# One transfer per cache page instead of two, in a hybrid decoder step with paged latent attention

## The chip, the cores and the metric

The kernel runs on one core of a Trainium2 chip. Times are device microseconds (us) of one execution. The median of three runs of the kernel before is 3482.98 us (3482.84 to 3485.76). The five engines are TensorE (PE), VectorE (DVE), ScalarE (ACT), GpSimd (POOL) and SyncE (SP, which here only issues transfers); all transfers run on the core's 16 DMA engines.

## The reference, cut to what matters

One decoder layer serves a prompt of 1024 tokens and 8 sample sequences of one new token each. The prompt and the samples share all weights. After the mixer comes an expert retrieval: every token picks 128 of 16384 experts, and a row of 1024 floats is gathered for each pick from two tables (`expert_u`, `expert_v`). The part that the change touches is the samples' attention over their cache:

```python
past_ckv = cache_ckv[l, page_table].reshape(dec_b, past, KV_RANK)      # 16 pages of 128 keys, 256 floats each
past_kr = cache_krope[l, page_table].reshape(dec_b, past, QK_ROPE)     # the same keys, 64 floats each
s = (jnp.einsum('bqhr,bkr->bhqk', q_lat, ckv)
     + jnp.einsum('bqhp,bkp->bhqk', q_rope, kr)).astype(jnp.float32) * SM_SCALE
p = jax.nn.softmax(s, axis=-1)
o_lat = jnp.einsum('bhqk,bkr->bqhr', p, ckv)
```

Each of the 8 samples has 16 pages of 128 keys, scattered in a pool by `page_table`; all data are float32.

## The kernel before, in words

**The backbone.** The expert retrieval of the 8 prompt tiles (128 tokens each) is the long work. Each tile has 32 groups of 4 picks, so there are 256 groups. For a group GpSimd issues 4 gathers into `u_ring` and 4 into `v_ring` (L1854, each 128 rows of 4 KB; each ring has 8 slots), VectorE forms 4 dot products (L1737), ScalarE the gelu and four diagonals (L1223), and TensorE adds the weighted rows up in 16 matmuls (`v_group`, L925). A gather waits until its slot is free: `u_free` comes from VectorE's dot product, `v_free` from TensorE's matmuls.

**The front work.** All else (projections, attention, mixing, top-k of the next tile or of the samples) is cut into stages. `make_plan` spreads them over the groups by a table of costs; every engine's program has the same order. The samples are the last unit: their stages lie in groups 195 to 249. Of these, 36 are stages of `pages`, numbered n, four for each sample b (a quarter of its pages each) and four to drain. A stage of pages n = 4b + q works on TensorE like this: scores of the quarter before (L840, L841), `page_turn` (transposes of the quarter's 4 pages, L862 for the latents and L863 for the rope keys), the scores turned (L853), and, where q is 2, `page_values` of the sample before (L879 to L884), whose end is the event `page_pv`. VectorE and ScalarE copy the transposed pages out (L1524, L1525, L1157). In a group with stages of pages, VectorE does two of the group's four dot products ahead of the stage and two behind it, and TensorE does one stage ahead of its `v_group`. Some groups have two stages.

**The loads.** SP issues all page loads in order (`load_page`, L534 to L538): it reads the page number from `page_table_sb` into a register and issues the transfers. Even and odd samples have different homes. For sample 0 the 16 latent pages are loaded early, when the prompt's attention is over; its 16 rope pages go to `w_ukT`, which the samples' own queries still need, and so they are issued only once `qlat_kept`, `q_roped`, `conv_done` and `conv_stored` have come. Then follow samples 1 to 7, each with 16 pages of two transfers, 128 rows of 1024 bytes and 128 rows of 256 bytes; sample b waits for `page_pv` of sample b - 2, which had the same home. `page_turn` waits for a whole quarter:

```python
pe.wait_ge(pages_loaded[b % 2][q], (b // 2 + 1) * 2 * QP * 16)
```

The homes before are `ckv_rows` and `ckvT` (latents, even samples), `w_ukT` (rope keys, even samples) and `work` (odd samples, latents and rope keys apart). Behind the page loads SP has the weights of the samples' output and query projections.

Of the kernel before, what the change touches and what calls it, by code (L numbers as in the profile page):

```python
# [26 lines left out]
P = 128  # L27
# [3 lines left out]
TILES = SEQ // P  # L31
SB = 8
PAGE = 128
NPAGES = 16
# [3 lines left out]
ROPE = 64  # L38
QR = 384
KV = 256  # L40
# [31 lines left out]
QP = NPAGES // QUARTERS  # L72
# [189 lines left out]
def build(nc, a, out):  # L262

    with ExitStack() as ctx:
        def sb(name, shape, dt=F32):
            return ctx.enter_context(nc.sbuf_tensor(name, shape, dt))
# [5 lines left out]
        pages_loaded = [[ctx.enter_context(nc.semaphore(f"pages_loaded{i}{q}")) for q in range(QUARTERS)] for i in range(2)]  # L272
# [3 lines left out]
        F = [ctx.enter_context(nc.psum_tensor(f"front{i}", [P, 512], F32)) for i in range(6)]  # L276

        ident = sb("ident", [P, P])
# [9 lines left out]
        w_uq = sb("w_uq", [P, QR // P, H, NOPE + ROPE])  # L288
        w_ukT = sb("w_ukT", [P, H, KV])
# [3 lines left out]
        ckv_rows = sb("ckv_rows", [P, TILES, KV])  # L293
        ckvT = sb("ckvT", [P, 2, SEQ])
# [16 lines left out]
        work = sb("work", [P, 5 * D])  # L311
# [38 lines left out]

        second_keys = [W[1][:, h * 256:(h + 1) * 256] for h in range(4)] + [mix_raw[:, h * 256:(h + 1) * 256] for h in range(1, 4)] + [W[2][:, 256:512]]

        prompt_keys = [ckv_rows[:, :, :], ckvT[:, :, :].rearrange("p c (n r) -> p (c n) r", r=KV)]
        pages_kr = [w_ukT[:, :, :].rearrange("p h (n r) -> p (h n) r", r=ROPE),
                    work[:, NPAGES * KV:NPAGES * (KV + ROPE)].rearrange("p (n r) -> p n r", r=ROPE)]

        def page_rows(b, n):
            if b % 2:
                return work[:, n * KV:(n + 1) * KV]
            return prompt_keys[n // TILES][:, n % TILES, :]  # L360

        pages_T = rows_next[:, :, :].rearrange("p a b -> p (a b)")[:, 0:3 * 512].rearrange("p (c k) -> p c k", c=3)

# [82 lines left out]
        def _(sp):  # L446
# [19 lines left out]
            r = 0  # L466
            for name in ("g_mix_norm", "g_q", "g_kv", "g_attn_out", "g_conv_out"):
                n = a[name].shape[1] // P
# [5 lines left out]
            def load_rope(u):  # L474

                after(sp, on.q_roped, UNITS[u][0])
                row, T = UNITS[u][0] * P, width(u)
                sp.dma_start(cos_t[:, 0:T], a["c_rope"][0, :, row:row + T]).then_inc(on.rope_loaded, 16)
                sp.dma_start(sin_t[:, 0:T], a["c_rope"][1, :, row:row + T]).then_inc(on.rope_loaded, 16)
# [50 lines left out]
                load_unit_start(u)  # L530
                load_unit_rest(u)

            def load_page(b, n, what):
                page = sp.value_load(page_table_sb[0:1, b * NPAGES + n:b * NPAGES + n + 1], min_val=0,  # L534
                                     max_val=a["cache_ckv"].shape[1] - 1)
                for dst, src in what:
                    sp.dma_start(dst, a[src][0, bass.ds(page, 1)].rearrange("a k r -> k (a r)"))\
                        .then_inc(pages_loaded[b % 2][n // QP], 16)  # L538


            sp.wait_ge(on.olat_kept, TILES * H)
            sp.wait_ge(on.pages_table_loaded, 16)
            for n in range(NPAGES):
                load_page(0, n, [(page_rows(0, n), "cache_ckv")])
            load_rope(SAMPLE)
            load_unit_start(SAMPLE)
            for k in range(CONV, N_IN + WR):
# [4 lines left out]
            sp.wait_ge(on.q_roped, TILES + 1)  # L552
            sp.wait_ge(on.conv_done, SAMPLE + 1)
            sp.wait_ge(on.conv_stored, 3 * 16)
            for n in range(NPAGES):
                load_page(0, n, [(pages_kr[0][:, n, :], "cache_krope")])
            for b in range(1, SB):

                if b >= 2:
                    sp.wait_ge(on.page_pv, b - 1)  # L560
                for n in range(NPAGES):
                    load_page(b, n, [(page_rows(b, n), "cache_ckv"), (pages_kr[b % 2][:, n, :], "cache_krope")])
            for k in range(N_IN + WR, PIECES):
                load_w(SAMPLE, k)

# [12 lines left out]
        def _(pe):  # L578
# [277 lines left out]

            def page_turn(n):
                b, q = divmod(n, QUARTERS)
                pe.wait_ge(pages_loaded[b % 2][q], (b // 2 + 1) * 2 * QP * 16)
                for pg in range(QP):  # L860
                    for c in range(2):
                        nc.tensor.transpose(F[c][:, pg * P:(pg + 1) * P], page_rows(b, q * QP + pg)[:, c * P:(c + 1) * P], ident[:])  # L862
                    last = nc.tensor.transpose(F[2][0:ROPE, pg * P:(pg + 1) * P], pages_kr[b % 2][:, q * QP + pg, :], ident[:])  # L863
                last.then_inc(on.page_turned, 1)

            def own_key_scores():
# [21 lines left out]
            def pages_stage(n):  # L888

                b, q = divmod(n, QUARTERS)  # L890
                if n == 0:
                    own_key_scores()
                if q == 1 and b:
                    pe.wait_ge(on.page_max_made, 2 * b - 1)
                    nc.tensor.transpose(F[5][0:H, 0:P], small_col(C_PM, 4), ident[:]).then_inc(on.page_gmax, 1)
                if 0 < n <= SB * QUARTERS:
                    page_scores(n - 1)
                if n < SB * QUARTERS:
                    page_turn(n)
                if q == 1 and b:  # L900
                    pe.wait_ge(on.page_max_made, 2 * b)
                    nc.tensor.matmul(F[5][:, 128:132], gm_rows[:], ident[0:H, 0:H], start=True, stop=True)\
                        .then_inc(on.page_gmax_spread, 1)
                if 0 < n <= SB * QUARTERS:
                    page_scores_turn(n - 1)
                if q == 2 and b:
                    page_values(b - 1)
                if q == 3 and b:
                    pe.wait_ge(on.value_rows_kept, b)
                    for c in range(2):  # L910
                        last = nc.tensor.matmul(F[5][:, COLS_VALUES + 4 * c:COLS_VALUES + 4 * c + 4],
                                                value_rows[:, c * P:(c + 1) * P], pick_values[:], start=True, stop=True)
                    last.then_inc(on.values_turned, 1)
# [124 lines left out]
            for t in range(SB):  # L1038
                pe.wait_ge(v_loaded[t], (TILES * (GROUPS // 2) + 1) * 16)
                for q in range(4):  # L1040
                    last = nc.tensor.matmul(acc[32 * q:32 * q + SB, 0, 0:256], s_fan[:, t, :], v_ring[:, t, q * 256:(q + 1) * 256],
                                            start=(t == 0), stop=(t == SB - 1))
# [910 lines left out]
```

## Time and profile before

| | |
|---|---|
| median of three runs | 3482.98 us |
| the profiled execution | 3482.97 us |
| its span, first to last instruction | 3481.2 us |
| busy: PE, DVE, POOL, ACT | 72%, 65%, 66%, 24% |
| moved by DMA | 1279.47 MB in 368,936 packets, mean 368 GB/s |
| mean granted TensorE clock | 0.83 of full speed |
| first transfer into a home of a page | 2436 us |
| first rope page of sample 0 issued | 2771.5 us |
| last page values (`page_values` of sample 7) done | 3153.6 us |

The span is what the engines' instructions cover; the 1.8 us between it and the execution's own time lie around it. A packet of the DMA view is one row of a transfer (4 KB for a gather, 1024 or 256 bytes for a page) or one write of a semaphore, 16 of them for each transfer.

### The profile page before, as it was taken

How to read it: one execution, taken by the hardware profiler on the slowest of the kernel's cores; microseconds unless marked ns; L12 is line 12 of the kernel's file. 1: busy time of each engine (PE TensorE's matmuls, PEld its weight loads, DVE VectorE, ACT ScalarE, POOL GpSimd, SP SyncE). 2: the span in 40 equal slices, each digit the busy share in tenths (PEclk: the TensorE clock that was granted, in tenths of full speed). 3: DMA queues.
4: the chain of work that ended last, by engine and by line, in shares of the span. 5: the costliest groups of instructions: out<-in, count | busy, mean ns of one | idle time of the engine just before them, and what ended most of it. 6: DMA issues, size and time to landing. Idle time of an engine off the chain costs nothing.

```text
span 3481.2 us, 38789 instructions
## 1 busy us (share of the span) xinstructions
PE 2504.6 (72%) x11520; PEld 1399.3 (40%) x11520; DVE 2277.3 (65%) x5456; ACT 823.2 (24%) x2065; POOL 2291.3 (66%) x2068
## 2 busy tenths in 40 slices
PE   7558764977874497788854878878655888877764
PEld 6425432644541154444511544445213534432421
DVE  3685588467588955665898557657897254454784
ACT  2112222233222121332212213322112122232111
POOL 0467566666567775676777777676677576557675
PEclk9878878999987798899976999989876688888676
DMA  6699999998999999999999999999999999999998
GB/s 239 234 400 365 354 404 372 353 365 307 403 370 359 372 388 382 327 359 407 409 374 384 388 411 357 329 411 410 403 356 383 361 368 353 342 341 403 411 409 339
DMA packets 368936, 1279.47 MB, mean 368 GB/s; under 512 B 59372, under 2 KB 77974, under 8 KB 353368
## 3 DMA queue, kind: packets, MB, share of 16 engines
q0 software_dynamic: 297216, 1082.26, 81.2%
q1 hardware_dynamic: 62324, 168.67, 12.6%
q10 hardware_dynamic: 9188, 26.05, 2.3%
q8 instruction: 95, 1.56, 0.2%
q14 instruction: 113, 0.93, 0.1%
HBM read 1262.31 MB, written 13.48 MB: 366 GB/s over the span
## 4 chain that ended last, share of the span: by engine, by line
DVE 36%; PE 35%; DMA 13%; issue 7%; ACT 4%; POOL 2%; SPq 2%; DVEq 0%; ACTq 0%; POOLq 0%
DVE u_ring L1737 14%; PE acc L925 11%; PE front L587 10%; DMA u_ring<-in_expert_u,pick_cur 6%; PE front L803 3%; DMA v_ring<-in_expert_v,pick_cur 2%; DVE si_u L1604 2%; DVE sv L1603 2%; PE front L712 2%; PE front L735 2%; DVE work L1604 2%; DMA w_ukT<-in_cache_krope 1%; DVE work L1603 1%; DVE work L1648 1%; DVE work L1650 1%
## 5 line engine op out<-in xcount | busy, mean ns | idle before, releaser
L925 PE MATMUL acc<-v_ring,diag 128*64 128x512 f32 x4096 | 1176.1, 723 | 623.1 <-ACT diag L1223 354.7
L1854 POOL DMA_INDIRECT u_ring<-in_expert_u,pick_cur x1024 | 1144.0, 1117 | 576.8 <-issue 293.4
L1854 POOL DMA_INDIRECT v_ring<-in_expert_v,pick_cur x1024 | 1130.6, 1104 | 587.8 <-PE acc L925 313.3
L1737 DVE CUSTOM_DVE_ANT_0 u_ring<-u_ring,xn_cur 128x1024 f32<-128x1024 f32 x1024 | 1209.6, 1221 | 318.3 <-DMA u_ring<-in_expert_u,pick_cur 302.7
L925 PEld LDWEIGHTS acc<-v_ring,diag 128*64 128x64 f32 x4096 | 347.8, 165 | 1328.7 <-issue 905.6
L1223 ACT ACTIVATE diag<-ident,wgt 128x64 f32<-128x64 f32 x1024 | 272.3, 337 | 759.4 <-DVE wgt L1743 707.9
L587 PE MATMUL front<-work,w_ring 128*128 128x256 f32 (+2 forms) x1536 | 308.9, 343 | 25.2 <-DVE mo L1596 14.5
L587 PE MATMUL front<-mo,w_ring 128*128 128x256 f32 (+2 forms) x1536 | 304.2, 339 | 0.0
L587 PEld LDWEIGHTS front<-work,w_ring 128*128 128x128 f32 x1536 | 254.2, 204 | 77.1 <-issue 36.1
L1216 ACT ACTIVATE gelu<-dots 128x4 f32<-128x4 f32 x256 | 52.5, 205 | 922.8 <-DVE dots L1737 922.7
L587 PEld LDWEIGHTS front<-mo,w_ring 128*128 128x128 f32 x1536 | 259.0, 205 | 22.6
L803 PE MATMUL front<-w_ring,work 128*128 128x256 f32 (+1 forms) x512 | 120.2, 396 | 18.5 <-DVE work L1569 14.2
L1603 DVE MAX8 sv<-work 128x8 f32<-128x128 f32 (+1 forms) x252 | 72.5, 288 | 84.3 <-ACT work L1201 27.3
L1524 DVE COPY rows_next<-front 128x512 f32<-128x512 f32 x32 | 22.1, 691 | 141.2 <-PE front L863 141.2
L803 PEld LDWEIGHTS front<-w_ring,work 128*128 128x128 f32 (+1 forms) x512 | 93.9, 186 | 50.8 <-DVE work L1569 15.9
L1216 ACT ACT_TABLE_LOAD x85 | 109.1, 1283 | 1.5
L735 PE MATMUL front<-work,ckv_rows 128*128 128x128 f32 x560 | 79.9, 305 | 26.3 <-DVE work L1508 26.3
L735 PEld LDWEIGHTS front<-work,ckv_rows 128*128 128x128 f32 x560 | 74.2, 215 | 39.1 <-DVE work L1508 32.4
L1737 DVE DVE_READ_ACCUMULATOR2_ANT dots<- 128x1 f32 x1024 | 82.8, 81 | 0.0
L712 PE MATMUL front<-ckvT,rows_next 128*128 128x512 f32 (+3 forms) x176 | 72.6, 537 | 9.2 <-DVE q_ro L1425 5.8
L1604 DVE FIND_INDEX8 si_u<-sv,work 128x8 uint32<-128x128 f32 (+1 forms) x252 | 71.5, 284 | 0.6 <-issue 0.6
L1603 DVE MAX8 work<-mo 128x8 f32<-128x256 f32 (+1 forms) x144 | 61.4, 426 | 15.5 <-DVE mo L1625 0.9
(303 smaller groups left out, 2329.1 us busy)
## 6 DMA issues: line engine op xcount, KB each, us to landing
w_ring<-in_w_pieces SPq DMA_DIRECT2D x112, 1024.0 KB
u_ring<-in_expert_u,pick_cur POOLq DMA_INDIRECT x1024, 10.1
v_ring<-in_expert_v,pick_cur POOLq DMA_INDIRECT x1024, 9.1
x_t<-in_x_prompt SPq DMA_DIRECT2D x16, 512.0 KB
v_ring<-in_w_pieces SPq DMA_DIRECT2D x8, 1024.0 KB, 11.9
work<-in_cache_ckv SPq DMA_DIRECT2D x64, 128.0 KB
xn_cur<-scratch ACTq DMA_DIRECT2D x14, 512.0 KB, 10.0
scratch_x<-rows_next ACTq DMA_DIRECT2D x8, 512.0 KB
```

The costliest lines, as they stand in the source:

```text
L587: last = nc.tensor.matmul(dst, w[:, k, c0:c0 + m], x_chunks(k // 4)[:, (k % 4) * T:(k % 4 + 1) * T], start=(k == 0), stop=(k == DC - 1))
L712: nc.tensor.matmul(dst, q_lat[:, c, h, :], ckvT[:, c, ks], start=(c == 0), stop=False)
L735: last = nc.tensor.matmul(F[4][:, c * P:(c + 1) * P], ckv_rows[:, j, c * P:(c + 1) * P], W[1][:, j * P:(j + 1) * P], start=(j == 0), stop= ...
L803: last = nc.tensor.matmul(dst, mixed[i][:, k * T:(k + 1) * T], w[:, k, :], start=(k == 0), stop=(k == DC - 1))
L925: last = nc.tensor.matmul(acc[rows, half, :], diag[:, s % RING, :], v_ring[:, s % RING, half * 512:half * 512 + 512], start=(s < 2), stop= ...
L1216: nc.scalar.activation(gelu[:, g * G:(g + 1) * G], dots[:, g * G:(g + 1) * G], ACT.Gelu).then_inc(on.gelu_done, 1)
L1223: nc.scalar.activation(diag[:, s % RING, :], ident2[:], ACT.Copy, scale=wgt[:, s:s + 1]).then_inc(on.diag_made, 1)
L1603: own(v.max(best, scores), held=True)
L1604: last = v.max_index(index[:, 8 * r:8 * r + 8], best, scores)
L1648: own(v.tensor_tensor(hit[0:T], pos_f[0:T, c, hs].unsqueeze(3).to_broadcast(grid), iota16[0:T].unsqueeze(1).unsqueeze(1).to_broadcast(grid ...
L1737: v.tensor_tensor_reduce(u_ring[:, slot, :], u_ring[:, slot, :], xn2_cur[:, block_of(r), :], 1.0, 0.0, ALU.mult, ALU.add, dots[:, g * G + ...
L1854: pool.indirect_dma_start(ring[:, slot, :], None, a[table][0], bass.IndirectOffsetOnAxis(ap=pick, axis=0)).then_inc(loaded[slot], 16)
```

## The change

The host lays `cache_ckv` and `cache_krope` side by side in one input `cache_rows`, so that a key's 256 latents and 64 rope values are one row of 1280 bytes. A page is then one transfer of 128 such rows. In the core's memory a page takes 320 columns. Odd samples have all 16 in `work`. Even samples have six in `ckv_rows`, six in `ckvT` and four in `w_uq`. The first twelve pages of sample 0 are loaded early; its last four wait for the events that the rope pages waited for. The bytes are the same.

```diff
+        PAGE_COLS = KV + ROPE
+        HELD_PAGES = TILES * KV // PAGE_COLS
+        page_homes = [ckv_rows[:, :, :].rearrange("p n r -> p (n r)"), ckvT[:, :, :].rearrange("p c t -> p (c t)"),
+                      w_uq[:, :, :, :].rearrange("p c h n -> p (c h n)")]
+
+        def page_at(b, n):
+
+            if b % 2:
+                return work[:, n * PAGE_COLS:(n + 1) * PAGE_COLS]
+            home, k = divmod(n, HELD_PAGES)
+            return page_homes[home][:, k * PAGE_COLS:(k + 1) * PAGE_COLS]
...
-            def load_page(b, n, what):
+            def load_page(b, n):
                 page = sp.value_load(page_table_sb[0:1, b * NPAGES + n:b * NPAGES + n + 1], min_val=0,
-                                     max_val=a["cache_ckv"].shape[1] - 1)
-                for dst, src in what:
-                    sp.dma_start(dst, a[src][0, bass.ds(page, 1)].rearrange("a k r -> k (a r)"))\
-                        .then_inc(pages_loaded[b % 2][n // QP], 16)
+                                     max_val=a["cache_rows"].shape[0] - 1)
+                sp.dma_start(page_at(b, n), a["cache_rows"][bass.ds(page, 1)].rearrange("a k r -> k (a r)"))\
+                    .then_inc(pages_loaded[b % 2][n // QP], 16)
...
-            for n in range(NPAGES):
-                load_page(0, n, [(page_rows(0, n), "cache_ckv")])
+            for n in range(2 * HELD_PAGES):
+                load_page(0, n)
...
-            for n in range(NPAGES):
-                load_page(0, n, [(pages_kr[0][:, n, :], "cache_krope")])
+            for n in range(2 * HELD_PAGES, NPAGES):
+                load_page(0, n)
...
-                    load_page(b, n, [(page_rows(b, n), "cache_ckv"), (pages_kr[b % 2][:, n, :], "cache_krope")])
+                    load_page(b, n)
...
-                pe.wait_ge(pages_loaded[b % 2][q], (b // 2 + 1) * 2 * QP * 16)
+                pe.wait_ge(pages_loaded[b % 2][q], (b // 2 + 1) * QP * 16)
...
+    arrays["cache_rows"] = np.concatenate([arrays["cache_ckv"][0], arrays["cache_krope"][0]], axis=2)
```

`page_rows` and `page_kr` are now the first 256 and the last 64 columns of `page_at`. No matmul, copy or wait of another engine changes in kind or number.

## Rows read from the trace of the kernel before

**Rows 1.** The page's 40 slices (87 us each) of the whole execution

```profile
DMA  6699999998999999999999999999999999999998
GB/s 239 234 400 365 354 404 372 353 365 307 403 370 359 372 388 382 327 359 407 409 374 384 388 411 357 329 411 410 403 356 383 361 368 353 342 341 403 411 409 339
```

**Rows 2.** Busy time by stretch: us, busy us and count per engine, PEclk, DMA, GB/s

```profile
2771.00:3153.00 382.00, 304.56 (x1623) 145.94 (x1620) 191.60 (x403) 102.45 (x244) 244.53 (x219) 0.84 0.98 352
3200.00:3400.00 200.00, 135.93 (x574) 65.34 (x574) 145.69 (x390) 34.33 (x112) 140.64 (x132) 0.72 1.03 410
```

**Rows 3.** DMA view, 3200 to 3400 us

```profile
DMA packets 21224, 82.06 MB, mean 410 GB/s; under 512 B 2365, under 2 KB 2365, under 8 KB 20060
```

**Rows 4.** DMA view, 2855 to 2867 us, with two queues

```profile
DMA packets 2233, 4.73 MB, mean 395 GB/s; under 512 B 726, under 2 KB 1237, under 8 KB 2231
...
q0 software_dynamic: 1116, 4.07, 86.6%
q1 hardware_dynamic: 1115, 0.65, 17.8%
```

**Rows 5.** DMA view, 2780 to 2784 us, then 2444 to 2448 us

```profile
DMA packets 820, 1.59 MB, mean 397 GB/s; under 512 B 456, under 2 KB 456, under 8 KB 820
...
DMA packets 688, 1.59 MB, mean 397 GB/s; under 512 B 69, under 2 KB 379, under 8 KB 687
```

**Rows 6.** DMA view, 2771 to 3153 us

```profile
DMA packets 66219, 134.44 MB, mean 352 GB/s; under 512 B 23732, under 2 KB 38068, under 8 KB 66189
...
q0 software_dynamic: 31197, 113.62, 79.3%
```

**Rows 7.** DMA view, 2831 to 2843 us, then 3023 to 3035 us

```profile
DMA packets 1043, 3.81 MB, mean 317 GB/s; under 512 B 114, under 2 KB 114, under 8 KB 1043
...
DMA packets 1074, 1.88 MB, mean 157 GB/s; under 512 B 427, under 2 KB 703, under 8 KB 1073
```

**Rows 8.** Waits, 2771 to 3153 us: engine line waited for: us, times, longest

```profile
POOL u_ring L1854 <- DVE dots L1737: 57.8, 11, 8.4
PE front L862 <- DMA w_ukT<-in_cache_krope: 34.4, 7, 7.2
...
PE front L862 <- DMA work<-in_cache_krope: 14.7, 4, 4.4
```

**Rows 9.** TensorE's timeline: a quarter of sample 3's pages, two of sample 5's

```profile
2908.37 0.69 PE L862 MATMUL front<-ident,work 128*128 128x128 f32 x2 [4.45 <-DMA work<-in_cache_krope]
...
3008.24 0.44 PE L862 MATMUL front<-ident,work 128*128 128x128 f32 x2 [4.30 <-DMA work<-in_cache_krope]
...
3020.55 0.69 PE L862 MATMUL front<-ident,work 128*128 128x128 f32 x2 [4.00 <-DMA work<-in_cache_krope]
```

**Rows 10.** TensorE's timeline, one stage of pages at full clock

```profile
2918.39 1.05 PE L840 MATMUL front<-rows_next 128*32 128x512 f32 x4
...
2923.11 3.65 PE L925 MATMUL acc<-v_ring,diag 128*64 128x512 f32 x16
```

**Rows 11.** Timeline of SP's queue: issue of page transfers

```profile
2435.96 8.51 SPq L537 DMA_DIRECT2D ckv_rows<-in_cache_ckv  x8
...
2771.53 17.27 SPq L537 DMA_DIRECT2D w_ukT<-in_cache_krope  x16
...
2789.57 0.62 SPq L537 DMA_DIRECT2D work<-in_cache_ckv  x1
...
2845.28 0.34 SPq L537 DMA_DIRECT2D ckv_rows<-in_cache_ckv  x1
...
2846.89 0.34 SPq L537 DMA_DIRECT2D ckv_rows<-in_cache_ckv  x1
...
2894.27 0.34 SPq L537 DMA_DIRECT2D work<-in_cache_ckv  x1
```

**Rows 12.** GpSimd's timeline, one gather

```profile
2836.38 0.94 POOL L1854 DMA_INDIRECT v_ring<-in_expert_v,pick_cur  x1 [0.30 <-issue]
```

**Rows 13.** The chain that ended last, 2771 to 3153 us, shares by line

```profile
by line: DMA w_ukT<-in_cache_krope 12.6%; PE acc L925 11.2%; SPq L537 10.7%; issue 8.1%; DMA work<-in_cache_krope 7.0%; PE front L862 5.8%; DMA v_ring<-in_expert_v,pick_cur 5.4%; SPq L534 5.1%; DVE u_ring L1737 4.9%; PE front L882 4.2%; PE 
```

More of the change, by code:

```diff
@@ L351, in build, with page_kr @@
         second_keys = [W[1][:, h * 256:(h + 1) * 256] for h in range(4)] + [mix_raw[:, h * 256:(h + 1) * 256] for h in range(1, 4)] + [W[2][:, 256:512]]
-        prompt_keys = [ckv_rows[:, :, :], ckvT[:, :, :].rearrange("p c (n r) -> p (c n) r", r=KV)]
-        pages_kr = [w_ukT[:, :, :].rearrange("p h (n r) -> p (h n) r", r=ROPE),
-                    work[:, NPAGES * KV:NPAGES * (KV + ROPE)].rearrange("p (n r) -> p n r", r=ROPE)]
+        PAGE_COLS = KV + ROPE
[7 more added lines that the diff above has]
+            return page_homes[home][:, k * PAGE_COLS:(k + 1) * PAGE_COLS]
         def page_rows(b, n):
-            if b % 2:
-                return work[:, n * KV:(n + 1) * KV]
-            return prompt_keys[n // TILES][:, n % TILES, :]
+            return page_at(b, n)[:, 0:KV]
+        def page_kr(b, n):
+            return page_at(b, n)[:, KV:PAGE_COLS]
         pages_T = rows_next[:, :, :].rearrange("p a b -> p (a b)")[:, 0:3 * 512].rearrange("p (c k) -> p c k", c=3)
@@ L862, in page_turn @@
                         nc.tensor.transpose(F[c][:, pg * P:(pg + 1) * P], page_rows(b, q * QP + pg)[:, c * P:(c + 1) * P], ident[:])
-                    last = nc.tensor.transpose(F[2][0:ROPE, pg * P:(pg + 1) * P], pages_kr[b % 2][:, q * QP + pg, :], ident[:])
+                    last = nc.tensor.transpose(F[2][0:ROPE, pg * P:(pg + 1) * P], page_kr(b, q * QP + pg), ident[:])
                 last.then_inc(on.page_turned, 1)
@@ L1943 @@
     arrays["w_pieces"] = w_pieces
-    for name in ("w_in", "w_o", "w_query"):
+    arrays["cache_rows"] = np.concatenate([arrays["cache_ckv"][0], arrays["cache_krope"][0]], axis=2)
+    for name in ("w_in", "w_o", "w_query", "cache_ckv", "cache_krope"):
         del arrays[name]
```

## The prediction

> **What bounds the kernel now.** I read the slices of the page first, then the busy time of the stretches, the DMA view of short windows, the waits, and last the timelines of TensorE and of SP's queue.
>
> The slices show a kernel that lives near the DMA engines' limit: from the third slice on the DMA row is mostly nines, and the best slices move 400 to 411 GB/s [rows 1]. Where is the real ceiling? From 3200 to 3400 us the core holds 410 GB/s while every other engine has time left [rows 2, 3], so this is the rate of full DMA engines with large rows. In the stretch of the pages, 2771 to 3153 us, the DMA share looks as full (0.98), but only 352 GB/s are moved [rows 2]. The reader should see here that the share counts time that packets are open, not work done. To tell how full the engines are I price a packet.
>
> Take r bytes per ns and h ns for each packet, on one of 16 engines. Rows 3: 82.06 MB / r + 21,224 h = 200 us x 16 = 3200 us. Rows 4: 4.73 MB / r + 2233 h = 12 x 16 = 192 us. Solved: r = 27.0 and h = 7.5 ns. Two windows that I did not use agree: both stretches of [rows 5] come out at 64 to 65 us of work in 4 x 16 = 64. So a 4 KB row costs 159 ns, a 1024-byte row 45.5, a 256-byte row 17.0, a write of a semaphore 7.5.
>
> With these prices the whole page stretch holds 134.44 / 27.0 + 66,219 x 7.5 ns = 5480 us of work on 16 engines, that is 342.5 us in 382: the DMA engines stand idle for 39.5 us [rows 6]. One window where no page is loading is 22% idle, and the one from 3023 us, where the gathers had run dry, 59% [rows 7]. After 3153 us there is almost no idle time until the end [rows 2, 3], so whatever is saved before goes straight into the result.
>
> Why the idle time? TensorE waits 34.4 + 14.7 = 49.1 us for rope pages at L862, and GpSimd 57.8 us for VectorE's dot products [rows 8]: two of them stand behind the stage, whose copies wait for `page_turn`. A late page stops TensorE, then VectorE, then the gathers. The chain says the same: transfers of rope pages and SP's issue of pages (L534, L537) are 35% of it [rows 13].
>
> Why are pages late? In rows 4 the gathers' queue q0 and SP's queue q1 moved 1116 and 1115 packets: the engines take the two queues in turn, packet by packet, whatever their size. A page of two transfers is 288 packets, so beside gathers it takes 288 / 1115 x 12 = 3.10 us, and a quarter 12.4. TensorE's waits for two neighbouring quarters end 12.3 us apart [rows 9]. A sample's 16 pages need 49.6 us, while a stage of pages at full clock takes 4.72 + 3.65 = 8.4 us [rows 10], four of them 34. Issue is no limit beside that: 1.6 us for a page with two transfers [rows 11]. Pages are late because small rows waste turns.
>
> **The change part by part.**
>
> Packets. 128 pages lose 128 rows and 16 semaphore writes each: 18,432 x 7.5 ns / 16 = **8.6 us** of DMA work. The bytes stay. No row shows a packet of 1280 bytes; by r and h it costs 54.9 ns, between the 45.5 of 1024 bytes (below it cannot cost less) and the 45.5 + 17.0 = 62.5 of the two rows that it replaces. I take 54.9, since the same line passes through 4 KB and 1 KB rows. At 62.5 only the semaphore writes are saved, 1.0 us; at 45.5 the saving would be 18. By the Trainium skill's "DMA: Bandwidth & Descriptors", section "Anatomy of one DMA — SWDGE (gpsimd) path" (fitted to GpSimd's transfers), a DMA has some 2.0 us fixed beside its bytes; 128 fewer would be worth 256 us if they stood in a row. The trace speaks against it: sixteen rope transfers were issued in 17.3 us [rows 11], one upon the other, so the fixed part overlaps.
>
> Turns. A page is now 144 packets. A turn of both queues took 12 x 16 / 1115 = 172 ns; the page packet's mean grows from 29 to 50 ns, so a turn is 192 ns and a page takes 9 turns on each engine, **1.73 us** for 3.10. A quarter takes 6.9 us, a sample 27.7. The first quarter: sample 3's was issued at 2894.27 and let TensorE go at 2908.37 [rows 9, 11], 14.1 us, or 12.4 + 1.7. It becomes 6.9 + 1.7 = 8.6. It is wanted after `page_values`: two `v_group` of 3.65, a stage of 4.7 and the scores 2.0, that is 14.0 us, or 10.3 where two stages share a group. Later quarters come every 6.9 us and are wanted every 8.4. So I count the 49.1 us of waits for pages as gone.
>
> Sample 0. Before, TensorE waited at stage 0 for rope pages issued from 2771.5 us. Now quarters 0 to 2 are there, and quarter 3 is issued in 4 x 1.16 = 4.6 us instead of 17.3 [rows 11]. Sample 1's loads start at about 2777 instead of 2789.6 [rows 11]. That wait is in the 49.1.
>
> Issue and queues. SP's MOVE, register load and one DMA take 1.16 us a page, from eight latent pages in 9.3 us [rows 11] (they end 8.51 us after 2435.96), for 1.6 before. Issue is under service (1.73), so SP does not limit. Early, SP issues 12 for 16 and reaches the next weights 4.6 us sooner; nobody waits for these. GpSimd's queue is untouched.
>
> Early loads. 12 x 0.447 = 5.4 us of DMA work replace 16 x 0.372 = 5.9, in a stretch that is full [rows 5]; this is in the 8.6. New homes. `w_uq` is last read by the samples' `q_proj`, before `qlat_kept`; TensorE's transposes and values read as many columns of the same shape from other places, so I cost them at nothing; should they take longer, TensorE has slack (below).
>
> Idle time. The 39.5 us do not all go. While pages load, both queues have work and the engines are full [rows 4]; 7 x 27.7 + 7 = 201 us of that. In the other 155 us or so only gathers run. GpSimd issues one each 1.24 us [rows 12], hardly faster than the 1.28 us that it costs, and any hiccup is lost. How idle are they? Between the 8% of the middle slices (about 375 against 410 GB/s [rows 1]) and the 22% of [rows 7]. Halfway, 15%, is 23 us (12 to 34). Saved: 39.5 - 23 = **17 us** (6 to 27). Does TensorE become the bound? The stretch's 31,197 packets of q0 [rows 6] are 27 groups of 8 gathers, 3.0 for each of nine samples' worth of stages. At full clock TensorE needs 3.0 x 3.65 + 4 x 4.7 + 3 for the values = 33 us a sample, DMA 3.0 x 8 x 1.28 + 16 x 0.447 = 38. It does not, with 5 us to spare.
>
> Sum: 8.6 + 17 = 26 us off the profiled execution's 3482.97 us, which is the median of the runs to 0.01: **3457 us**.
>
> **The rivals.**
>
> Packets only (15%). The waits for pages turn into waits for gathers and the idle time stays. For it: gathers, once late, stay late with rings of 8. Against: idle time came where pages stopped the consumers. 3483 - 8.6 = 3474 us.
>
> All idle time gone (10%). Both queues always have work; 8.6 + 27 to 39.5 gives 3435 to 3447. Against: the window without pages of [rows 7].
>
> No change (9%). The stretch is bound by bytes, not by packets or waits: 134.44 MB stay, 352 GB/s stay, 3483 us. Or the 1280-byte row is served as two and the saved idle is made elsewhere. Against bytes: 410 GB/s for 200 us [rows 3]. The Trainium skill, "DMA: Bandwidth & Descriptors", section "Where 436 GB/s comes from", has some 358 GB/s as what binds a load from HBM; by that rule the stretch would already be at its limit and the time stay. The 410 GB/s disagree.
>
> Slower (6%). In a burst of pages a gather pays 9 turns of 192 instead of 172 ns, 0.18 us more, 1.45 a group; two groups in each of seven bursts are 20 us. If the gathers do not win that back between bursts, the time is 3483 - 8.6 + 20 = 3495. It decides once idle time grows by over 15.6 us (8.6 + 7). Against: bursts are shorter, and between them a gather costs 1.28 instead of 1.55 us.
>
> **How the numbers follow.** The likeliest case (60%) has 3457, its own range is 3447 to 3468 from the bounds 6 and 27 of the idle time. The range 3440 to 3475 takes in most of the packets-only case and about half of the one without idle time, near 8 in 10. 0.2% is 7 us, about what a measurement of this kernel tells from nothing. Faster: 60 + 14 + 10 = 84%; same: 9 + 1 = 10%; slower 6%.
>
> **What would show it.** Right: TensorE waits for pages under 5 us in all; 18,432 fewer packets; the stretch near 356 us; equal packet counts of q0 and q1 while a sample loads, for some 28 us; GpSimd's wait for dot products well under 57.8. Wrong: waits of L862 for `cache_rows` of tens of us (a page needs far more than 1.73 us), or idle DMA time near 40 us without them, with GpSimd's issue or `v_free` as what holds the gathers.

## The result and the profile after

The changed kernel takes 3455.97 us (median of 4 runs, 3454.71 to 3463.55), the kernel before 3484.37 in the same count of runs (3482.84 to 3486.85). The ratio on record is 0.9911 with the interval 0.9891 to 0.9932: about 0.9% faster. It is not the quotient of the two medians, which is 0.9918 and lies inside the interval; the difference is 2.6 us. The prediction was 3457 us, its range 3440 to 3475. The profiled execution took 3456.30 us with a span of 3454.4.

The page of the changed kernel: the slices and the packets of the whole execution, beside [rows 1].

```profile
span 3454.4 us, 38357 instructions
...
DMA  6699999999999999999999999999999999999998
GB/s 240 236 398 357 351 398 368 350 362 327 372 368 361 371 383 408 331 339 395 411 392 367 374 411 372 336 390 411 407 385 362 398 368 400 400 355 400 411 409 339
DMA packets 350499, 1279.41 MB, mean 370 GB/s; under 512 B 40940, under 2 KB 59542, under 8 KB 334936
```

368,936 packets have become 350,499: the 18,432 that the change takes away and 5 others. The megabytes are the same within 0.1. In the slices the reader should look at numbers 32 to 36, which hold the pages. They moved 361, 368, 353, 342 and 341 GB/s before and move 398, 368, 400, 400 and 355 now; the last four are within 3 of what they were.

The stretch of pages runs from the first late page of sample 0 to the end of `page_values` of sample 7: before 2771.5 to 3153.6 us (382), now 2774.7 to 3125.9 (351.2). Busy time of this stretch and of the full one behind it, columns as in [rows 2]; then the DMA view of 2774 to 3126 us, beside [rows 6]:

```profile
2774.70:3125.90 351.20, 295.08 (x1622) 135.25 (x1618) 192.86 (x402) 102.48 (x244) 252.92 (x219) 0.90 1.01 384
3200.00:3400.00 200.00, 136.92 (x562) 66.34 (x562) 145.67 (x386) 30.08 (x107) 142.63 (x134) 0.70 1.03 410
```

```profile
DMA packets 48494, 135.02 MB, mean 384 GB/s; under 512 B 5380, under 2 KB 20228, under 8 KB 48468
...
q0 software_dynamic: 31332, 114.11, 84.2%
```

By the prices of the prediction (27.0 bytes per ns, 7.5 ns a packet) the stretch of 351.2 us holds about 335 us of work: 16 us idle, where before some 39 were. (Work is not measured: it is bytes and packets times these prices.) The share in the DMA column hardly moved (0.98 to 1.01), but the bytes did (352 to 384 GB/s). TensorE's granted clock, a mean over its two levels of 1.2 and 2.4 GHz, went from 0.84 to 0.90 of full speed here, in a stretch in which the engine stops less often for long. Its busy time fell from 304.56 to 295.08 us for as many instructions (1623 and 1622). No run changes the clock and the waits apart, so how much of the shorter stretch goes through the clock stays open.

The waits of the stretch, TensorE's and then GpSimd's, beside [rows 8]:

```profile
PE acc L935 <- DMA v_ring<-in_expert_v,pick_cur: 27.0, 16, 4.5
...
PE front L872 <- DMA work<-in_cache_rows: 2.4, 1, 2.4
...
PE front L872 <- DMA ckv_rows<-in_cache_rows: 1.2, 1, 1.2
```

```profile
POOL u_ring L1864 <- DVE dots L1747: 22.0, 6, 8.4
```

The reader should see that TensorE's 49.1 us of waits for pages are 3.6 now, and that it waits instead for gathered rows (27.0 us), as one would expect where the DMA engines are full. GpSimd's wait for dot products fell from 57.8 to 22.0. The chain has changed in the same way; beside [rows 13], SP's lines and the pages are gone from its head:

```profile
by line: DMA v_ring<-in_expert_v,pick_cur 19.1%; PE acc L935 16.0%; issue 11.3%; DVE u_ring L1747 6.9%; DMA u_ring<-in_expert_u,pick_cur 6.0%; PE front L872 5.2%; POOL u_ring L1864 4.5%; PE front L850 4.4%; PE front L851 4.4%; POOL v_ring L
```

The DMA view of 12 us in which a sample's pages load beside gathers, beside [rows 4]; and of 12 us without pages, beside [rows 7]:

```profile
DMA packets 1999, 4.77 MB, mean 398 GB/s; under 512 B 224, under 2 KB 1111, under 8 KB 1999
...
q0 software_dynamic: 1000, 3.64, 77.3%
q1 hardware_dynamic: 999, 1.14, 26.3%
```

```profile
DMA packets 1017, 3.70 MB, mean 309 GB/s; under 512 B 114, under 2 KB 114, under 8 KB 1016
```

One packet of a page for one of a gather, as before. (So even are the windows in which both queues have work all the time; from 2786.67 us, early in sample 1's load, 12 us have 1360 of q1 and 869 of q0.) A turn of both queues takes 12 x 16 / 999 = 192 ns, the predicted value, so that 9 turns, a page, take 1.73 us.

SP's timeline, issue of pages, beside [rows 11]; and TensorE's first transposes of sample 0:

```profile
2774.67 3.68 SPq L547 DMA_DIRECT2D w_uq<-in_cache_rows  x4
...
2779.11 17.21 SPq L547 DMA_DIRECT2D work<-in_cache_rows  x16
...
2842.82 5.83 SPq L547 DMA_DIRECT2D ckv_rows<-in_cache_rows  x6
...
2849.42 5.85 SPq L547 DMA_DIRECT2D ckvT<-in_cache_rows  x6
...
2856.04 3.99 SPq L547 DMA_DIRECT2D w_uq<-in_cache_rows  x4
...
2882.13 16.85 SPq L547 DMA_DIRECT2D work<-in_cache_rows  x16
```

```profile
2777.31 0.44 PE L872 MATMUL front<-ident,ckv_rows 128*128 128x128 f32 x2
```

Issue takes 17.2 us for sample 1's 16 pages, where it took 27.5; they start 4.4 us after the first late page of sample 0 instead of 18.0, and the first stage's transposes start 2.6 us after SP's first late page instead of 9.2.

### The profile page after: what moved, and what is told of

Same layout as the page of the kernel before. It is cut to its first block, busy times and chain, and to the rows that moved or that the text cites. A ratio compares the mean times of both kernels' runs of the same rounds, so it can differ in the third digit from the quotient of the medians.

```text
span 3454.4 us, 38357 instructions
## 1 busy us (share of the span) xinstructions
PE 2494.0 (72%) x11520; PEld 1390.7 (40%) x11520; DVE 2281.1 (66%) x5456; ACT 823.4 (24%) x2065; POOL 2300.4 (67%) x2068
## 2 busy tenths in 40 slices
DMA packets 350499, 1279.41 MB, mean 370 GB/s; under 512 B 40940, under 2 KB 59542, under 8 KB 334936
## 4 chain that ended last, share of the span: by engine, by line
DVE 34%; PE 32%; DMA 18%; issue 8%; ACT 4%; POOL 3%; DVEq 0%; ACTq 0%; SPq 0%; POOLq 0%
DVE u_ring L1747 14%; PE acc L935 10%; DMA u_ring<-in_expert_u,pick_cur 9%; PE front L597 8%; DMA v_ring<-in_expert_v,pick_cur 6%; PE front L813 3%; DVE si_u L1614 2%; POOL u_ring L1864 2%; PE front L722 2%; DVE sv L1613 2%; DVE work L1614 1%; PE front L745 1%; POOL v_ring L1864 1%; DVE work L1613 1%; DVE work L1658 1%
## 5 line engine op out<-in xcount | busy, mean ns | idle before, releaser
L1864 POOL DMA_INDIRECT v_ring<-in_expert_v,pick_cur x1024 | 1144.4, 1118 | 583.2 <-PE acc L935 312.5
L1747 DVE CUSTOM_DVE_ANT_0 u_ring<-u_ring,xn_cur 128x1024 f32<-128x1024 f32 x1024 | 1211.6, 1222 | 345.8 <-DMA u_ring<-in_expert_u,pick_cur 338.9
```

Of the source, the lines that this page charges most:

```text
L1747: v.tensor_tensor_reduce(u_ring[:, slot, :], u_ring[:, slot, :], xn2_cur[:, block_of(r), :], 1.0, 0.0, ALU.mult, ALU.add, dots[:, g * G + ...
L1864: pool.indirect_dma_start(ring[:, slot, :], None, a[table][0], bass.IndirectOffsetOnAxis(ap=pick, axis=0)).then_inc(loaded[slot], 16)
```

## The experiments

Each was compared with the kernel before on its own chip; there the kernel before had medians from 3484.8 to 3486.7 us, with single runs between 3471 and 3498. So the ratios are what to compare; like the one above, they differ by up to 0.0014 from the quotients of the medians. The changed kernel itself has 0.9911. "Work" and "idle" are of the stretch of pages, by the prices above, within 0.3 us by rounding; "waits" are TensorE's for pages.

| run | ratio | interval | stretch | work | idle | waits |
|---|---|---|---|---|---|---|
| before | 1 | | 382.1 | 342.7 | 39.3 | 49.1 |
| changed | 0.9911 | 0.9891 to 0.9932 | 351.2 | 334.9 | 16.3 | 3.6 |
| two_rows | 0.9993 | 0.9974 to 1.0013 | 378.8 | 344.3 | 34.5 | 47.8 |
| two_halves | 0.9999 | 0.9984 to 1.0014 | 377.8 | 343.6 | 34.3 | 44.2 |
| by_keys | 1.0044 | 1.0024 to 1.0063 | 385.7 | 336.8 | (48.9) | 14.0 |
| even_keys | 0.9910 | 0.9880 to 0.9941 | 356.9 | 336.9 | 20.0 | 6.7 |
| slow_issue | 0.9927 | 0.9897 to 0.9957 | 355.7 | 337.1 | 18.6 | 8.2 |
| late_first | 0.9921 | 0.9896 to 0.9946 | 358.1 | 340.2 | 17.9 | 10.9 |
| dots_ahead | 1.0026 | 1.0006 to 1.0045 | 381.0 | 348.3 | 32.7 | 48.0 |
| after_dots_ahead | 0.9923 | 0.9899 to 0.9947 | 347.4 | 338.9 | 8.5 | 3.9 |
| extra_packets | 0.9938 | 0.9915 to 0.9961 | 357.9 | 343.9 | 14.0 | 3.0 |
| four_parts | 1.0152 | 1.0124 to 1.0179 | 435.7 | 366.3 | 69.4 | 91.6 |

The theory is that of the prediction: the number of packets makes the gain, by their own 7.5 ns and by the turns that they take from a queue that alternates with the gathers. The rivals are the homes with the early start, and the number of transfers that SP issues.

### Two transfers in the new homes

```diff
-                sp.dma_start(page_at(b, n), a["cache_rows"][bass.ds(page, 1)].rearrange("a k r -> k (a r)"))\
-                    .then_inc(pages_loaded[b % 2][n // QP], 16)
+                for c0, c1 in ((0, KV), (KV, PAGE_COLS)):
+                    sp.dma_start(page_at(b, n)[:, c0:c1], a["cache_rows"][bass.ds(page, 1)].rearrange("a k r -> k (a r)")[:, c0:c1])\
+                        .then_inc(pages_loaded[b % 2][n // QP], 16)
```

The wait of `page_turn` counts both. The second kernel is the same with `((0, 160), (160, 320))`.

> The new homes and the early twelve pages stay, but a page comes in two transfers again, 128 rows of 1024 and 128 of 256 bytes: 288 packets a page as before the change. If packets and turns make the gain (theory), most of it is lost: DMA work 8.6 us up, the idle time of the page stretch back near 39.5 us less some 5 for sample 0's start, so 3474 to 3483 us, and TensorE waits 35 to 50 us for pages. If the homes and the early start make it (rival), the time stays within 3 us of 3456.

> A page in two transfers of 128 rows of 640 bytes: 288 packets, no row under 512 bytes. If it is the number of packets that counts, 7.5 ns and one turn each whatever their size (theory), the time equals that of the run with 1024 and 256 bytes within 3 us, 3474 to 3483. If rows of 256 bytes cost something of their own (rival), it lies near 3460.

Medians 3480.42 and 3487.30 us, ratios 0.9993 and 0.9999: nearly all of the gain is gone, though homes and early pages are those of the change. The waits for pages of the first and of the second kernel:

```profile
PE front L873 <- DMA work<-in_cache_rows: 23.3, 5, 6.9
...
PE front L873 <- DMA ckvT<-in_cache_rows: 14.1, 4, 6.9
...
PE front L873 <- DMA ckv_rows<-in_cache_rows: 8.6, 2, 6.4
```

```profile
PE front L873 <- DMA work<-in_cache_rows: 19.9, 5, 7.4
...
PE front L873 <- DMA ckvT<-in_cache_rows: 17.0, 5, 7.5
...
PE front L873 <- DMA ckv_rows<-in_cache_rows: 7.0, 1, 7.0
```

With `w_uq` they are 47.8 and 44.2 us. The homes are not what makes the gain. The two kernels have the same packets and bytes but no rows of 256 bytes in the second; their ratios differ by 0.0006, inside both intervals, so rows of 256 bytes as such are not the cause. (The second kernel's 3487.30 lies above the 3483 that was expected and 6.9 us above the first, where 3 were expected. The kernel before had 3486.71 on that chip.) Both kernels also have twice as many transfers as the changed one; the next pair takes that apart.

### Two transfers by keys

In place of the same two lines (`HB` is 64):

```diff
+                for k0 in (0, HB):
+                    sp.dma_start(page_at(b, n)[k0:k0 + HB, :], a["cache_rows"][bass.ds(page, 1)].rearrange("a k r -> k (a r)")[k0:k0 + HB, :])\
+                        .then_inc(pages_loaded[b % 2][n // QP], 16)
```

> A page in two transfers of 64 keys each, rows of 1280 bytes: SP issues twice as often, as before the change, but a page has only 160 packets instead of 144. If packets and turns make the gain (theory), it is kept but for 10 turns instead of 9: 128 x 16 x 7.5 ns / 16 = 1.0 us of work and some idle time, 3456 to 3461 us. If it was the number of transfers that SP issues and the queue holds (rival), it is lost: 3475 to 3483.

3497.37 us, slower than the kernel before, and neither expectation. Waits for pages were only 14.0 us, where the kernels with 288 packets a page have 44 to 48. The second form takes `range(2)` for `k0` and `[k0:P:2, :]` on both sides, the even and the odd keys.

> A page in two transfers again, now the even and the odd keys, rows of 1280 bytes, 160 packets. The run with the first and the last 64 keys apart was slower than the kernel before with few waits for pages but only 335 GB/s while pages loaded. If that was the 64 neighbouring partitions written at once, this one, which writes every second of all 128, moves about 395 GB/s and has the ratio 0.990 to 0.995 (theory). If two transfers a page cost the gain whatever their packets (rival), it is 0.998 or more.

3453.43 us, 0.9910. The DMA view of 2895 to 2907 us of both kernels, first by halves, then by even and odd keys:

```profile
DMA packets 1731, 4.05 MB, mean 338 GB/s; under 512 B 271, under 2 KB 961, under 8 KB 1730
...
q0 software_dynamic: 866, 3.15, 79.8%
q1 hardware_dynamic: 864, 0.88, 23.6%
```

```profile
DMA packets 2025, 4.78 MB, mean 399 GB/s; under 512 B 307, under 2 KB 1108, under 8 KB 2025
...
q0 software_dynamic: 1028, 3.76, 79.3%
q1 hardware_dynamic: 997, 1.03, 24.3%
```

In both the queues take turns, but a turn costs 12 x 16 / 865 = 222 ns in the first and 190 in the second, at nearly the same bytes a packet. So in these runs the turns of pages written into 64 neighbouring partitions are longer by a sixth, and those of pages written into every second partition are not. The figure in brackets in the table is therefore not idle time: the prices do not hold there. For the question asked, the second run is the clean one: two transfers a page, 160 packets, the whole gain. SP issued 32 of them in 29.8 us.

### Slow issue

```diff
             def load_page(b, n):
+                sp.value_load(page_table_sb[0:1, n:n + 1], min_val=0, max_val=a["cache_rows"].shape[0] - 1)
                 page = sp.value_load(page_table_sb[0:1, b * NPAGES + n:b * NPAGES + n + 1], min_val=0,
```

> The changed kernel, but SP reads a page number from the table twice for every page, so that issue takes 1.7 to 1.9 us a page, no faster than the two transfers of before (1.6), with the transfers as they are. If packets and turns make the gain, little is lost, since a page's service beside gathers is 1.73 us anyway: ratio to the kernel before 0.990 to 0.994. If SP's shorter issue makes it (rival), the gain is gone: 0.998 to 1.002.

3454.53 us, 0.9927. SP's timeline of this kernel, sample 3:

```profile
2878.03 25.27 SPq L548 DMA_DIRECT2D work<-in_cache_rows  x16
```

Sixteen pages in 25.3 us, first issue to last, are 1.66 us a page, somewhat under the 1.7 to 1.9 that I expected. It is as slow as the fastest sample of the kernel before (sample 3, 25.5 us) and costs nothing that can be measured here. But in the kernel before SP's issue took longer for other samples: 27.5 and 26.6 us for samples 1 and 7, 34 to 38 us for samples 2, 4, 5 and 6, with single issues of 1.1 to 1.4 us instead of 0.34. No run has so slow an issue with 144 packets; the nearest is the one by even and odd keys, which took 30 us and kept the gain. So a faster issue than 1.6 us a page is not the cause; for the samples with 34 to 38 us, where the long issues may as well follow from the full queue, it is not tested apart.

### Sample 0 late

```diff
-            for n in range(2 * HELD_PAGES):
-                load_page(0, n)
...
-            for n in range(2 * HELD_PAGES, NPAGES):
+            for n in range(NPAGES):
```

> The changed kernel with all 16 pages of sample 0 loaded late, none early. Theory: its first quarter lands some 8.6 us after the first issue, so TensorE waits 5 to 7 us at the first stage, sample 1's pages start 14 us later and wait little: 3459 to 3468 us. The rival that the early homes make the gain says 3475 to 3483.

3461.55 us, 0.9921. The wait for sample 0's first quarter is back:

```profile
PE front L870 <- DMA ckv_rows<-in_cache_rows: 9.0, 2, 7.7
```

7.7 us of it is one wait. The stretch is 6.9 us longer than in the changed kernel, 5.3 of it priced work, for the pages that moved into it from before; the ratio differs by 0.001, within the intervals. The early pages are worth a few us at most.

### The order of the dot products

```diff
-                    half = G // 2 if has_pages(stages) else G
+                    half = G
```

> The kernel before, with all four dot products of a group ahead of the stage of pages instead of two. If late pages cost time because VectorE's dot products behind the stage hold back the gathers (the path from wait to idle transfers as predicted), GpSimd's 57.8 us of waits for dot products shrink to under 20 and the time falls by 4 to 15 us, ratio 0.996 to 0.999. If TensorE's own wait at v_free does it alone, the ratio is 1.000 within 0.002.

> The same move of the dot products in the changed kernel, where hardly a page is late. Theory: 22 us of GpSimd's waits for dot products are left there, and the move brings 0 to 5 us, ratio 0.990 to 0.992. If the order of VectorE's work mattered by itself, this run would gain as much as the one on the kernel before.

On the kernel before: 3491.56 us, 1.0026, so slower, not 4 to 15 us faster. Its waits in the stretch:

```profile
POOL v_ring L1854 <- PE acc L925: 53.1, 16, 10.4
...
PE front L862 <- DMA w_ukT<-in_cache_krope: 29.3, 9, 7.1
...
POOL u_ring L1854 <- DVE dots L1737: 19.8, 5, 5.1
...
PE front L862 <- DMA work<-in_cache_krope: 18.7, 4, 5.8
```

The waits for dot products did fall, from 57.8 to 19.8 us, but GpSimd's wait for slots of `v_ring` rose from 20.3 to 53.1, and TensorE waits for pages as long as before. The path over VectorE, which the prediction named, is one of two, as these waits read. With the dot products moved away from it, TensorE, standing at `page_turn`, holds back the other half of the gathers (those into `v_ring`) by itself. What the path over VectorE costs alone no run shows, and the rival's 1.000 within 0.002 was missed too, by a little. On the changed kernel the move gave 3455.13 us, 0.9923, no difference to the change alone, though the idle time of its stretch was 8.5 us instead of 16.3.

### Packets that nobody waits for

```diff
                 elif name == "pages":
                     b, q = divmod(n, QUARTERS)
                     if n == 0:
                         act.wait_ge(on.x1_stored, TILES * 16)
+                    if n < SB * QUARTERS:
+                        for k in range(QP * n, QP * (n + 1)):
+                            act.dma_start(w_ukT[:, 0, :][:, 2 * k:2 * k + 2], a["c_ident"][:, 0:2]).then_inc(on.pages_table_loaded, 16)
```

At its end SP waits for these transfers too.

> The changed kernel with the saved packets put back where no page waits for them: ScalarE's queue issues, four in each stage of pages, 128 transfers of 128 rows of 8 bytes (18,432 packets with their semaphore writes) into a place that nobody reads. If the gain is 8.6 us of packets' work and some 20 of turns in SP's queue (theory), the work comes back and most of the rest stays: 8.9 us on top of the changed kernel and up to 6 more for a third queue that takes turns, ratio to the kernel before 0.993 to 0.996. If packets cost nothing by themselves and only SP's queue counts (rival), 0.991.

3463.58 us, 0.9938. The DMA view of its stretch with ScalarE's queue q10, and TensorE's waits:

```profile
DMA packets 66850, 134.88 MB, mean 377 GB/s; under 512 B 23804, under 2 KB 38652, under 8 KB 66823
...
q10 hardware_dynamic: 18864, 1.71, 4.4%
```

```profile
PE acc L936 <- DMA v_ring<-in_expert_v,pick_cur: 24.0, 16, 4.3
...
PE front L873 <- DMA work<-in_cache_rows: 3.0, 1, 3.0
```

The priced work is 343.9 us, 9.0 more than in the changed kernel, but that follows from the count and the price. What is measured: the waits for pages stay at 3.0 us, the stretch is 357.9 us, 6.7 longer than in the changed kernel, and the time is 0.0027 of 3485, or 9 us, above the change by the ratios (5 by the quotients of the medians). The intervals overlap, and each stretch is one execution. Whether so small a packet takes its 7.5 ns can be read from a window that is full, 2878.6 to 2890.6 us:

```profile
DMA packets 2464, 4.66 MB, mean 389 GB/s; under 512 B 1113, under 2 KB 1431, under 8 KB 2462
...
q10 hardware_dynamic: 939, 0.01, 4.6%
```

It is 4.66 MB / 27.0 + 2464 x 7.5 ns = 191 us of work in 192; without a price for the 939 packets of q10 it would be 184. So these packets cost time by themselves, although no page waits for them, and neither the waits nor the idle time come back with them.

### Four transfers a page

The list of columns becomes `((0, 80), (80, 160), (160, 240), (240, 320))`: rows of 320 bytes, 576 packets a page.

> The changed kernel with a page in four transfers of 128 rows of 320 bytes: 576 packets instead of 144, the bytes the same. Theory: 128 x 432 x 7.5 ns / 16 = 26 us more DMA work than the changed kernel, and a page takes 36 turns, 5.8 us beside gathers, so that TensorE waits for pages far more than 49 us and the idle time is at least that of before: 3505 to 3550 us, ratio 1.006 to 1.02. If the packets' number has reached its effect with 288 (rival), the ratio is that of two transfers, 0.999 to 1.001.

3536.67 us, 1.0152. TensorE's waits for odd and for even pages, the two largest:

```profile
PE front L873 <- DMA work<-in_cache_rows: 57.6, 9, 12.8
...
PE front L873 <- DMA ckvT<-in_cache_rows: 31.7, 3, 16.7
```

All waits for pages are 91.6 us and the idle time 69.4. From 2823.4 to 2835.4 us, beside gathers, q0 and q1 moved 1189 and 1191 packets, so that 36 turns, a page, take 5.8 us, as expected. So 144, 288 and 576 packets a page give waits of 3.6, 44 to 49, and 91.6 us.

### In search of a version better than both

In the changed kernel `"pages": 8` in the table `COST` was set to 10 and to 6.

> The changed kernel with a planned cost of 10 instead of 8 for a stage of pages, so that the 36 stages lie over more groups. The stretch's remaining idle time is 16 us, at its start, at the change of tile and behind the last load. Theory: pages are on time and spread wider, other stages closer: within 5 us of the changed kernel, ratio 0.989 to 0.993.

> The changed kernel with a planned cost of 6 for a stage of pages: the 36 stages lie closer, a sample has fewer groups. A page's service leaves room (1.73 us for 2.1 between stages' needs): within 5 us of the changed kernel, unless the first quarters are late again, then up to 10 slower.

3446.91 us with 0.9896 (0.9869 to 0.9922) and 3449.37 us with 0.9903 (0.9876 to 0.9931). The medians are 9 and 7 us under the changed kernel's, more than the 5 expected, but both ratios lie inside the changed kernel's interval, so neither is shown to be better. Idle time in their stretches is 7.0 us of 377 and 10.8 of 318.

## Why the prediction was right

**What bounds the kernel.** The DMA engines' work, priced by bytes and packets, was the right measure: a window that I had not used for the prices, with rows of 1280 bytes that did not exist before, comes out full. From 2895 to 2907 us it is 4.77 MB / 27.0 + 1999 x 7.5 ns = 192 us of 192. Behind the stretch nothing was given back: 327.6 us before, 328.5 now.

**Packets.** 8.6 us predicted. The run that put 18,432 packets back without anyone waiting for them was longer by 6.7 us in the stretch and by 9 by the ratios, and its full windows bear out 7.5 ns for a packet of 8 bytes; the total is not clear of the noise. The 1280-byte row costs what the line through the other rows said: at the 62.5 ns of the two rows that it replaced, the window of 2895 to 2907 us would hold 198 us of work in 192.

**Turns and waits.** A page in 1.73 us beside gathers, and 1.73 by the packet counts; waits under 5 us, measured 3.6. Two kernels with 288 packets in the new homes lose the whole gain, one with two transfers and 160 packets keeps it.

**Sample 0 and issue.** Both right in sign and small. Sample 1's loads were to start at about 2777 us, some 5 after the first late page; it was 4.4. But 1.6 us for a page of two transfers was read from two quick pages of sample 2, whose sixteen took 37.7 us by the trace, 2.4 a page.

**Idle time.** This term was mis-sized, and it was looked for in the wrong place. I kept 23 us and took 17 as saved; 16.3 were left and 23 saved. The prediction had the engines full while pages load and put all of the idle time that stays where only gathers run, 15% of some 155 us. Cut both stretches into pieces of 2 us, price the packets of each and part the pieces by whether SP's queue moves packets in them (more than 20). Before the change, pages were loading in 296 us of the stretch, and 28 of the 39 idle us lay there, 12 in the 86 us without. Now pages load in 206 us (201 forecast) with 7.5 us idle, and the 144 us without pages have 9, or 6% and not 15%. So 20 of the 23 us came from the time in which pages load. The window from 2904 to 2916 us of the kernel before shows how:

```profile
DMA packets 3332, 3.41 MB, mean 284 GB/s; under 512 B 1663, under 2 KB 2886, under 8 KB 3331
...
q1 hardware_dynamic: 2821, 1.58, 45.2%
q0 software_dynamic: 510, 1.82, 39.8%
```

The gathers have run dry behind a late page, SP's queue is nearly alone, and its small rows do not fill the engines: 9.5 us of work in 12. (By the prices a page of two transfers is 0.52 us of work, and SP issued this sample's at one in 1.6 us.) [rows 4] show turns beside gathers only; the second window of [rows 7], 59% idle, was already of this kind (654 of its packets are SP's). One window without pages, 3087 us, is still 25% empty (9.0 us of work in 12); others are 12 to 15% empty or full. So the stretch is 31 us shorter, not 25.

**Why the sum still fitted.** The stretch began 3.2 us later in the profiled execution than before, 2774.7 against 2771.5. Nothing shows that to be an effect of the change: among the twelve profiled kernels whose code up to there differs at most in how sample 0's pages are loaded, this start lies anywhere from 2768.3 to 2782.6 us, and the kernel with the old homes and other dot products has 2777.4. The error of the idle term, some 6 us, is about what single executions scatter. So it is in part luck that 3457 met 3456 to 1 us; between the medians lie 28 us, where 26 were forecast, and 31 by the ratio.

**The rivals.** Packets only would have kept 39 us of idle time; it fell to 16. All idle time gone did not come either. Bytes do not bind: the same bytes went at 384 instead of 352 GB/s, which is also above the 358 or so that the Trainium skill's "DMA: Bandwidth & Descriptors" gives as the limit in its section "Where 436 GB/s comes from". Gathers did lose in the bursts, 192 for 172 ns a turn, but the shorter stretch says that they won it back. One link of the chain was told too narrowly, as the waits of the dot product run on the kernel before say: VectorE's two dot products behind the stage were not needed for a late page to stop the gathers.

## What to carry to other kernels

Where a small transfer shares DMA engines with a stream of large ones, count its packets, not its bytes: here, while both queues had work, each packet of either let one of the other pass, so a page of 288 packets came at 3.1 us and one of 144 at 1.7. Where a late small transfer stops the stream, the small one alone does not fill the engines (a fifth of the time idle in the window above), and most of the idle time that was saved lay there. Price bytes and packets from two full windows, and look for windows where the priced work is less than the time, those with small transfers under way too; the busy share (0.98 and 1.01 here) does not show them. And a stall that is removed is worth the idle time of the bound engine that it caused, 23 us here, not the 45 us by which the wait shrank.

## What the runs showed of the hardware that was not expected

A transfer of 128 rows cut into the first and the last 64 partitions cost more than the two transfers by columns: while such pages loaded, the engines moved 338 GB/s at 222 ns a turn, against 399 GB/s and 190 ns with every second partition, and the kernel was 1.3% slower (1.0044 against 0.9910). The Trainium skill's "DMA: Bandwidth & Descriptors", section "The descriptor swizzle", says that in a transfer to 128 partitions each engine writes to a port of its own, the ports of partitions 0 to 63 being other ones than those of 64 to 127. That 64 neighbouring partitions would have to share fewer ports fits the two runs. But no run here looked at ports, and the two forms also differ in which rows of the page one transfer reads (64 in a row, or every second), so the cause stays open.
